# Norming x and the context apart, turning x between modulation steps, and loading constants and zeros later

## What is computed

```python
mod_x = (jax.nn.silu(c) @ w_ada[l] + b_ada[l])[:, None, :]
mod_c = jax.nn.silu(c_ctx) @ w_ada[l] + b_ada[l]
sh1, sc1, g1, sh2, sc2, g2 = jnp.split(mod_x, N_MOD, axis=-1)
...
p_x = modulate(rmsnorm(h, norm_mix_w[l]), sh1, sc1) @ w_in[l]      # h is x, 512 x 1024
p_c = modulate(rmsnorm(hc, norm_mix_w[l]), csh1, csc1) @ w_in[l]   # hc is ctx, 256 x 1024
```

## Time and profile before

| | us |
|---|---|
| three runs | 2194.8, 2199.06, 2198.26; median 2198.26 |
| the profiled execution: its time, its span | 2182.58, 2180.7 |
| PE busy in the span | 2087.6 (96%) |
| DVE, ACT, POOL busy | 974.0, 495.3, 218.2 |
| block 1, from the first PE instruction to PE's last | 13.16 to 217.67 |
| the fill of `y_scratch`, issue to landing | 103.3 |

### The profile page before, as it was taken

How to read it: one execution, slowest core, us unless ns; L and a number is a source line. 1 busy time by engine, 2 the same in 40 slices (tenths; PEclk the granted TensorE clock), 3 DMA queues, 4 the chain that set the end, 5 groups by cost and what they waited for, 6 DMA issues and landing times.

```text
span 2180.7 us, 36117 instructions
## 1 busy us (share of the span) xinstructions
PE 2087.6 (96%) x14969; PEld 1030.8 (47%) x14969; DVE 974.0 (45%) x1651; ACT 495.3 (23%) x878; POOL 218.2 (10%) x266
## 2 busy tenths in 40 slices
PE   5959899999999999999999999899999999999998
PEld 2824545333333333333333333688484448777643
DVE  2511535742232223223322345754577625597742
ACT  2400312111111011101110110311126102666560
POOL 1000001112211221122112222200000000000000
PEclk9979899999999999999999999999999999999999
DMA  9972325999999999999999999713121032212200
GB/s 376 337 293 91 146 109 229 415 412 424 418 415 420 423 418 420 423 420 423 418 421 417 421 421 418 286 69 109 39 105 50 1 105 78 97 58 97 97 20 39
DMA packets 111832, 565.90 MB, mean 259 GB/s; under 512 B 16933, under 2 KB 29010, under 8 KB 77938
## 3 DMA queue, kind: packets, MB, share of 16 engines
q1 hardware_dynamic: 88950, 512.93, 58.1%
q0 software_dynamic: 19584, 49.84, 6.4%
q10 hardware_dynamic: 3228, 2.17, 0.3%
HBM read 545.21 MB, written 37.62 MB: 267 GB/s over the span
## 4 chain that ended last, share of the span: by engine, by line
PE 79%; DVE 3%; DMA 3%; issue 1%; ACT 1%; ACTq 0%; POOL 0%; SPq 0%; POOLq 0%; DVEq 0%
PE ps L2425 30%; PE ps L461 11%; PE ps L2395 9%; PE ps L3964 5%; PE ps L2403 5%; PE ps L3863 4%; PE ps L449 3%; PE ps L1649 2%; PE ps L3843 2%; DMA ring<-in_w_gu 1%; PE ps L3395 1%; PE ps L3386 1%; DMA ring<-in_odd_w_in 1%; PE ps L3015 1%; PE ps L3059 1%
## 5 line engine op out<-in xcount | busy, mean ns | idle before, releaser
L2425 PE MATMUL ps<-ring,xeT 128*32 128x512 f32 x6144 | 668.1, 593 | 4.8 <-DMA ring<-in_w_gu 4.1
L2425 PEld LDWEIGHTS ps<-ring,xeT 128*32 128x32 f32 x6144 | 196.3, 110 | 447.2 <-issue 440.4
L2395 PE MATMUL ps<-ring,mT 128*32 128x512 f32 x2048 | 266.6, 592 | 0.0
L2164 DVE TENSOR_TENSOR mT<-ps,spread_bias 128x768 f32<-128x768 f32 x32 | 30.6, 957 | 433.8 <-PE ps L2425 433.8
L2102 ACT ACTIVATE mT<-mT 128x768 f32<-128x768 f32 x32 | 27.0, 843 | 851.0 <-DVE mT L2164 851.0
L461 PE MATMUL ps<-hT_late,ring 128*128 128x256 f32 x704 | 157.7, 383 | 0.4 <-issue 0.4
L2403 PE MATMUL ps<-ring,mT 128*32 128x256 f32 x2048 | 157.4, 379 | 0.0
L461 PEld LDWEIGHTS ps<-hT_late,ring 128*128 128x128 f32 x704 | 135.0, 192 | 22.4 <-issue 3.7
L2403 PEld LDWEIGHTS ps<-ring,mT 128*32 128x32 f32 x2048 | 66.6, 110 | 153.2 <-issue 153.2
L3964 PE MATMUL ps<-ring,mT 128*128 128x512 f32 x256 | 110.4, 592 | 0.0
L1924 POOL DMA_INDIRECT xe<-xn_scratch,idx x93 | 96.5, 1037 | 31.4 <-issue 29.7
(11 more groups left out here) (517 smaller groups left out, 2569.0 us busy)
## 6 DMA issues: line engine op xcount, KB each, us to landing
ring<-in_w_gu SPq DMA_DIRECT2D x128, 2048.0 KB, 11.1
ring<-in_w_down SPq DMA_DIRECT2D x128, 1024.0 KB, 11.5
y_scratch<-zeros POOLq DMA_DIRECT2D x1, 20352.0 KB, 103.3
ring<-in_even_w_in SPq DMA_DIRECT2D x18, 1024.0 KB, 9.3
ring<-in_w_ada SPq DMA_DIRECT2D x32, 512.0 KB, 11.7
ring<-in_odd_w_in SPq DMA_DIRECT2D x16, 1024.0 KB, 7.7
ring<-in_w_ada SPq DMA_DIRECT2D x8, 1024.0 KB, 17.6
ring<-in_w_in SPq DMA_DIRECT2D x8, 1024.0 KB, 20.7
```

The lines of the kernel that those rows point to most:

```text
L2395: mm = nc.tensor.matmul(quad(b, 2 * q + n), acted(k, q, src), w[:, kk, n * BANK:(n + 1) * BANK], start=first, stop=last)
L2425: mm = nc.tensor.matmul(quad(q, c), left(q), part_columns(w, c), start=start, stop=stop)
```

## The change

Four things, all in block 1:

1. The norm of x and that of the context are two chains: ACT sums x's squares when x has landed (it waits for the context's transfer only before the context's squares), roots them, DVE scales x; then the same for the context.
2. PE turns x between the modulation steps 3 to 6, two groups of 128 columns behind each (`turn_x`); ACT copies the turned x to `hT` without modulating it. When `mod1` and `amix` are there, DVE modulates `hT` in place, eight instructions of 128x512. The context is turned after the last step, three groups of 256 columns ahead of the modulation rows and one behind them, and ACT modulates it from PSUM. PE's L947 (L965 now) waits for each modulated piece instead of for all.
3. Of the constants only the identity (64 KB) is loaded first; the other 888 KB are issued behind tile 7 of the ring.
4. The fill of `y_scratch` waits for PE's first product of the second panel (`p_vp.p1`), and POOL waits for its landing in block 2 instead of block 1.

```diff
             @block.sync
             def _(sp):
-                vec_loads.on(sp.dma_start(cst[:], A["cst"]), 16)
+                vec_loads.on(sp.dma_start(ident, A["cst"][:, C_ID:C_ID + P]), 16)
                 sp.wait_ge(zeroed.sem, 2)
                 load_vectors(sp, 1)
+                stream.load(sp, 1, MIX_SLOTS)
+                wgk_loads.on(sp.dma_start(cst[:, C_ID + P:], A["cst"][:, C_ID + P:]), 16)
                 stream.load(sp, end_inputs - 4, MIX_SLOTS)
...
                 scol_zeroed.wait(pool)
-                pool.wait_ge(mod_ready.sem, 3)
+                p_vp.p1.filled(pool)
                 rows_zeroed.on(pool.dma_start(
                     y_dram.rearrange("r (h n) -> (r h) n", n=BANK).rearrange("(p a) n -> p a n", p=CAP),
                     zeros[0:CAP, :].unsqueeze(1).to_broadcast([CAP, (E + XB) * D // BANK, BANK])), 16)
-                rows_zeroed.wait(pool)
...
-                for k in range(KD):
-                    j = j_tr[k][0]
+                for k, j in enumerate(j_tr):
+                    act_out(act, j, hT[:, k, 0:T], bank(j.bank))
+                act.wait_ge(mod_ready.sem, 2)
+                for i, j in enumerate(j_trc):
                     j.filled(act)
-                    j.empty(nc.scalar.activation(hT[:, k, 0:T], bank(j.bank), ACT.Identity,
-                                                 bias=mod1[:, k, 0:1], scale=amix[:, k, 0:1]))
+                    for half in range(2):
+                        k = 2 * i + half
+                        ins = nc.scalar.activation(hT[:, k, T:], ps[:, j.bank, half * TC:(half + 1) * TC], ACT.Identity,
+                                                   bias=mod1[:, k, 1:2], scale=amix[:, k, 1:2])
+                    j.empty(ins)
...
-                for k in range(KD):
-                    j = j_tr[k][1]
-                    j.filled(dve)
-                    j.empty(nc.vector.tensor_scalar(hT[:, k, T:], bank(j.bank, TC), amix[:, k, 1:2],
-                                                    mod1[:, k, 1:2], ALU.mult, ALU.add))
-                for j in j_tr[-1]:
+                for k, j in enumerate(j_tr):
                     j.emptied_for(dve)
+                    h_ready.on(nc.vector.tensor_scalar(hT[:, k, 0:T], hT[:, k, 0:T], amix[:, k, 0:1], mod1[:, k, 0:1],
+                                                       ALU.mult, ALU.add))
+                h_ready.wait(dve)
...
+                    if 3 <= k < KD - 1:
+                        if k == 3:
+                            pe.wait_ge(xn_ready.sem, NT)
+                        turn_x(2 * k - 6)
+                        turn_x(2 * k - 5)
+                pe.wait_ge(xn_ready.sem, NT + NTC)
+                for i in range(3):
+                    turn_context(i)
                 turn_vector_rows(pe, j_rows, j_mod[0], mod_rows)
-                pe.wait_ge(xn_ready.sem, NT + NTC)
...
+                turn_context(3)
...
+                        if j is j_r:
+                            pe.wait_ge(h_ready.sem, NT + NTC + 1 + k)
+                        elif k % 2 == 0:
+                            j_trc[k // 2].emptied_for(pe)
                         mm = nc.tensor.matmul(quad(j.bank, k % 4, cols.stop - cols.start), wr[:, k, :], hT[:, k, cols],
                                               start=k < 4, stop=k >= 4)
...
                 for a in amat:
                     amat_zero.on(nc.gpsimd.memset(a, 0.0))
+                rows_zeroed.wait(pool)
```

More of the change, by code:

```diff
@@ L547, in vector_step @@
             return mm
-        def vector_tiles(pe, job):
-            for k in range(KD):
[L551 to L557, removed]
         def vector_between(pe, job):
@@ L626, in build @@
         mod_ready = signal("mod_ready")
+        h_ready = xn_ready
         j_vec = [psum.job(0, "dve")]
+        j_tr = [psum.job((2, 3, 0)[k % 3], "act") for k in range(KD)]
         j_rows = psum.job(4, "dve")
+        j_trc = [psum.job(b, "act") for b in (5, 6, 7)]
         j_mod = [psum.job(1, "dve")]
+        j_trc.append(psum.job(2, "act"))
         mod_rows = ptok[:, 2, :]
@@ L633, in build @@
         rows_loads = signal("rows_loads")
-        j_tr = []
-        for k in range(KD):
-            j_tr.append((psum.job(2 + k % 3, "act"), psum.job(5 + k % 3, "dve")))
+        context_loads = rows_zeroed
         j_r = psum.job(0, "dve")
@@ L745, in _ @@
                 rows_loads.on(pool.dma_start(res[:], A["x"][0].rearrange("(t p) n -> p t n", p=P)), 16)
-                rows_loads.on(pool.dma_start(xc[:], A["ctx"][0].rearrange("(t p) n -> p t n", p=P)), 16)
+                context_loads.on(pool.dma_start(xc[:], A["ctx"][0].rearrange("(t p) n -> p t n", p=P)), 16)
                 scol_zeroed.on(nc.gpsimd.memset(zeros[:], 0.0))
                 scol_zeroed.wait(pool)
-                pool.wait_ge(mod_ready.sem, 3)
+                p_vp.p1.filled(pool)
                 rows_zeroed.on(pool.dma_start(
@@ L768, in _ @@
                 scol_ready.on(nc.scalar.activation(scol[:, :, 1], vcol("c_ctx", 0, KD), ACT.Silu))
[L769 to L778, removed]
-                    j = j_tr[k][0]
-                    j.filled(act)
-                    j.empty(nc.scalar.activation(hT[:, k, 0:T], bank(j.bank), ACT.Identity,
-                                                 bias=mod1[:, k, 0:1], scale=amix[:, k, 0:1]))
+                act.wait_ge(rows_loads.sem, 16)
+                for first, end in ((0, NT), (NT, NT + NTC)):
+                    if first:
+                        act.wait_ge(context_loads.sem, 16)
+                    for t in range(first, end):
+                        if t:
+                            rms_sum.wait(act)
+                        rms_sum.on(nc.scalar.activation(junk[:], xtile(t), ACT.Square,
+                                                        accum_out=stat[:, t:t + 1]))
+                    act.wait_ge(rms_mean.sem, 2 if first else 1)
+                    rms_root.on(nc.scalar.activation(stat[:, 16 + first:16 + end], stat[:, 8 + first:8 + end], ACT.Sqrt))
+                for k, j in enumerate(j_tr):
+                    act_out(act, j, hT[:, k, 0:T], bank(j.bank))
+                act.wait_ge(mod_ready.sem, 2)
+                for i, j in enumerate(j_trc):
+                    j.filled(act)
+                    for half in range(2):
[3 more added lines that the diff above has]
+                    j.empty(ins)
                 def queries_and_keys(j, b):
@@ L814, in _ @@
                 j_vec[0].empty(nc.vector.tensor_copy(vec[:], bank(0, 3 * P)))
[L815 to L822, removed]
+                for first, end in ((0, NT), (NT, NT + NTC)):
+                    dve.wait_ge(rms_sum.sem, end)
+                    rms_mean.on(nc.vector.tensor_scalar(stat[:, 8 + first:8 + end], stat[:, first:end], 1.0 / D, EPS, ALU.mult,
+                                                        ALU.add))
+                    dve.wait_ge(rms_root.sem, 2 if first else 1)
+                    dve_step.on(nc.vector.reciprocal(stat[:, 24 + first:24 + end], stat[:, 16 + first:16 + end]))
+                    dve_step.wait(dve)
+                    for t in range(first, end):
+                        xn_ready.on(nc.vector.tensor_scalar(xtile(t), xtile(t), stat[:, 24 + t:25 + t], None, ALU.mult))
                 j_rows.filled(dve)
@@ L835, in _ @@
                 mod_ready.wait(dve)
-                mod_ready.on(nc.vector.memset(stat[:, 60:61], 0.0))
-                for k in range(KD):
-                    j = j_tr[k][1]
-                    j.filled(dve)
-                    j.empty(nc.vector.tensor_scalar(hT[:, k, T:], bank(j.bank, TC), amix[:, k, 1:2],
-                                                    mod1[:, k, 1:2], ALU.mult, ALU.add))
-                for j in j_tr[-1]:
+                for k, j in enumerate(j_tr):
                     j.emptied_for(dve)
+                    h_ready.on(nc.vector.tensor_scalar(hT[:, k, 0:T], hT[:, k, 0:T], amix[:, k, 0:1], mod1[:, k, 0:1],
+                                                       ALU.mult, ALU.add))
+                h_ready.wait(dve)
                 w = {b: arrived(dve, blocks(p_qkg, b)) for b in EARLY_ORDER}
@@ L920, in _, with turn_x, turn_context @@
                 pe.wait_ge(scol_ready.sem, 2)
-                vector_tiles(pe, j_rows)
-                turn_vector_rows(pe, j_rows, j_mod[0], mod_rows)
-                pe.wait_ge(xn_ready.sem, NT + NTC)
[L925 to L937, removed]
+                def turn_x(k):
+                    j = j_tr[k]
+                    j.open(pe)
+                    for t in range(NT):
+                        mm = nc.tensor.transpose(ps[:, j.bank, t * P:(t + 1) * P], xtile(t)[:, k * P:(k + 1) * P], ident)
+                    j.done(mm)
+                def turn_context(i):
+                    j = j_trc[i]
+                    j.open(pe)
+                    for q in range(4):
+                        mm = nc.tensor.transpose(ps[:, j.bank, q * P:(q + 1) * P],
```

(13 more changed lines are left out.)

## The result

The change makes the kernel slower: 2220.95 us (median of 4 runs) against 2198.66 us (median of 4), ratio 1.0099 with a 95% interval of 1.0074 to 1.0124. The forecast was 9 us faster. The profiled execution of the changed kernel has a span of 2218.8 us. Its total is not compared with that of before, whose profiled execution (2182.58 us) is one of those with the median of 2181.72; the stages are. Block 3 of the changed kernel starts at 306.9 us and that of before at 285.3: 21.6 us, which is the 22.3 us of the medians. So all that is lost is lost ahead of block 3, as far as two profiled executions tell.

A forecast was written before the change was run, and what follows sets the result against it. Experts run at their weights' pace, so only an earlier start counts; the stages ahead are mostly PE's or chains of waits. Terms: 7 + 20.6 - 10.9 - 5.0 - 2.7 = 9.0 us won, giving 2189; range 2171 to 2197.

The forecast's parts named there:

- The front: Start of block 1: last modulation step ends near 36.2, L947's successor starts at 43.4; 7 us arrive at the second product.
- second rival: Start of block 1: at PE's low clock the earlier start gives nothing; won 2 us, time 2196, chance 0.15.
- The second panel: Block 1: its first product, at 146.63 before, starts at 119.0 once the fill is out of the way; 27.6 us won.
- The fill: Blocks 1 and 2: issued at 127.9, over at about 230, lying over block 1's last tiles and block 2's first loads.
- The step that failed: End of block 1: second cluster ends at 201.0, PE starts block 2 near 202 while the fill runs until about 230.
- third rival: Block 2: its loads beside the fill lose more than the second cluster won; lost 4 us, time 2202, chance 0.08.
- The term that was mis-sized: Block 2's loads beside the fill: first `pool_mat` lands at 209.6, `g1b` and `g2b` at 224.8; 9 us of gain left.
- The round-robin rule: Loads beside the fill: DMA engines alternate between queues by packet, so a tile takes twice its free time; not adopted.
- first rival: Second cluster and block 2: the late fill costs little, SP's queue gets half; won 25 us, time 2173, chance 0.25.

## Why the prediction was wrong

- **The front: right.** The last step was forecast to end at 36.2 (36.3), L947's successor at 43.4 (44.4), 7 us to arrive at the second product (6.0). PE's granted clock was 1.00 from 30 to 36 us, so the second rival's condition didn't arise. Two sizes were off by 1 us: eight modulations take 3.74 us and not 2.8, and the last `w_in` block landed at 48.9 as before and not at 47.8.
- **The second panel: right.** Forecast at 119.0, measured 121.46; the cluster ahead of it waited no longer for the fill. The 0.6 us put there for the start of a busy queue is in no row.
- **The fill: nearly right.** Issued at 127.9 and over at about 230, measured 131.5 and 239.0. That it doesn't fit in the free stretch, and lies over the second cluster and block 2, was forecast.
- **The step that failed.** The forecast had PE in block 2 from 202 on, with the fill under way until 230: "the second cluster [...] ends at 201.0", then the loads of block 2 beside the fill, and "the fill is over long before block 2 ends". With POOL's drain in place PE can't be in block 2 while the fill is under way: the end of block 1 holds every engine until it has landed (PE passed at 239.6, the fill landed at 239.0). The kernel's wait was moved, the block's own was not. No row of before shows it, since there the written wait came first and the fill had landed at 145.4, 72 us before PE was done. It cost 31.8 us of PE's time, of which 15 us are on top of the next point, since most of the loads that block 2 would have waited for landed meanwhile. The forecast had put this wait at nothing. The rivals had no such case: the third, "slower", was the loads alone.
- **The term that was mis-sized.** Even without the drain the kernel is 6.5 us slower than before and not 9 faster. The first `pool_mat` was put at 209.6 and landed at 225.5, the gate rows at 224.8 and landed at 239.85. The last tile of the second cluster, put at 200.1, was late already, at 205.6. Behind it `w_pool` and the first `pool_mat`, 1.25 tiles, were to take 9.5 us, at 7.6 us for each tile, and took 19.9. The 7.6 came from two 1 MB tiles that landed 15.2 us behind the tile of 131.4, and I took it for the pace of the queue beside the fill. The queues in 132 to 146 us of the kernel before (packets, MB, share of 16 engines):

```profile
q1 hardware_dynamic: 1313, 2.81, 54.6%
q0 software_dynamic: 246, 0.97, 21.3%
```

and in 200 to 239 us of the run without the drain:

```profile
q1 hardware_dynamic: 2540, 5.30, 38.9%
q0 software_dynamic: 1034, 4.19, 31.8%
```

The pace was nearly right: SP's queue moved 0.136 MB a us in the second, and 7.6 us a tile is 0.138. While PE waited for the last 1.3 MB ahead of its product, from 205.6 to 225.5 us, the queue moved 3.43 MB, so at least 2.1 MB of that were of loads issued later. What is late is the last part of each load. For each of these transfers the trace has sixteen rises of its semaphore, with their times. Those of the first `pool_mat`: five from 200.5 to 201.7, ten from 209.9 to 218.7, the last at 225.5. Those of the fill beside it: five from 197.4 to 198.8, one at 212.0, six from 219.8 to 221.5, then 226.9, 236.8, 236.9 and 244.1. In the kernel before, with no fill under way, the sixteen of the first `pool_mat` came within 1.5 us. So the fill's sixteen parts end 47 us apart, those of a load beside it 25 us, and the load lands with its last, whatever the queue moves in sum. The two tiles of the earlier trace rows were complete at 146.5, as the fill ended (145.4), so the 15.2 us were no price of two tiles. That the parts are the shares of the 16 DMA engines fits; the rises don't say which engine, nor how many bytes each part had.

The third rival set the threshold at 232.8 for `g2b`, which landed at 239.85. So without the drain its outcome, given 0.08, is what happened. Its slow queue of 0.115 MB a us is not, but its low clock is: the granted clock was 0.50 of full where block 2 starts (208.8 to 212 us) and 1.00 at that place before, and L1348 took 6.10 us where L1329 took 3.67.
- **The round-robin rule** of the Trainium skill, by which the time would have been that of the first rival (DMA: Bandwidth & Descriptors, Queues, rings and completion order), is about the turns of one engine between its queues. It doesn't give the landing time of a load here: a 1 MB load took 34.0 us beside the fill because its last part came 24 us after its fifth. Whether each engine takes turns as the rule has it, no run here shows.

## What to carry to other kernels

Moving the wait for a long transfer isn't enough when the engine that issued it comes to the end of a block first: on POOL that end waits for the landing. Start such a transfer so that it lands before the block's last work, or in pieces laid into the stretches where the DMA engines idle; here two halves in such stretches turned 22 us lost into 23 us won. And a load beside a long transfer lands with its slowest part, so neither the rate of its queue nor the distance between two landings near that transfer's end tells when it will be there.

## What the runs showed of the hardware

- SP and POOL differ at the end of a block. In the kernel before, with the drain in place, SP issued the first `pool_mat` at 212.84 and it landed 8.4 us later, at 221.2, while PE had passed the end of block 1 by 218.89: a load of SP holds nobody there. In the changed kernel POOL's transfer held PE for 31.8 us, and with POOL's drain left out PE passed at 208.9 with that transfer under way.
- POOL can run another instruction while its transfer is under way: the memset ran at 134.32, the fill was over at about 239.
- The whole fill takes about as long whatever lies beside it: 103.3 us with 14.2 MB on SP's queue (before), 107.5 with 7.8 (changed), 113.3 with 13.0 (no drain), 99.3 with 6.9 (in block 2). The first five of its sixteen parts ended 66 to 73 us after the issue in these four, the last 32 to 47 us after the first. A half took 53.0 us, thirteen parts by 172.6 and the last at 185.4, so its end is thin. In the version with two halves, 140 to 166 us and 172 to 186 us:

```profile
q0 software_dynamic: 1856, 7.58, 95.6%
```

```profile
q0 software_dynamic: 99, 0.39, 9.4%
```

  0.29 MB a us in the first stretch, 0.03 in the second.
